# Seven output products in the last block of a hybrid decoder layer too

## The reference

```python
h = rmsnorm(x, norm_g)
proj = h @ w_in                       # 1024 -> q, k, v, gk_lr, gate_g, u, gate_p, q_m, gate_m
o_gla  = rmsnorm(gla_chunked(q, k, v, gk), gla_norm_g) * silu(gate_g)   # 4 heads, 512 channels
o_pool = (pooled @ pool_w) * pool_scale * silu(gate_p)                  # 256 channels
o_mem  = memory_attention(q_m, mem_n, w_mem_kv) * silu(gate_m)          # 256 channels
mixed = concat([o_gla, o_pool, o_mem])                                   # 4096 x 1024
x = x + mixed @ w_out
return rmsnorm(x, final_g)
```

## Time and profile before

| | us |
|---|---|
| median of 3 runs | 1352.45 (1351.65 to 1354.74) |
| the profiled execution | 1352.88 |
| its span, first to last instruction | 1351.1 |
| TensorE busy | 1328.5 |
| VectorE busy | 921.9 |
| ScalarE busy | 817.1 |
| GpSimd busy | 450.7 |
| block 14 starts on TensorE | 1163.36 |
| block 15 (the last) starts | 1242.49 |
| the tail's first matmul | 1324.42 |

### The profile page before, as it was taken

How to read it: one execution, slowest core, us unless ns; L and a number is a source line. 1 busy time by engine, 2 the same in 40 slices (tenths; PEclk the granted TensorE clock), 3 DMA queues, 4 the chain that set the end, 5 groups by cost and what they waited for, 6 DMA issues and landing times.

```text
span 1351.1 us, 35800 instructions
## 1 busy us (share of the span) xinstructions
PE 1328.5 (98%) x14667; PEld 1003.7 (74%) x14667; DVE 921.9 (68%) x1664; ACT 817.1 (60%) x1481; POOL 450.7 (33%) x353
## 2 busy tenths in 40 slices
PE   6999999999999999999999999999999999999998
PEld 5788668577695877859687695968769596886954
DVE  6886667575656757666676857667685766758556
ACT  7886645655647466565655656566574756657353
POOL 2111164136522335243353432335343233534100
PEclk9999999999999999999999999999999999999999
DMA  9575656664673847747595877768596675858631
GB/s 386 190 209 200 243 187 216 209 227 192 216 256 115 330 155 240 260 125 300 186 305 173 280 256 212 263 186 307 183 280 246 211 267 185 311 188 280 251 92 49
DMA packets 155997, 302.92 MB, mean 224 GB/s; under 512 B 76112, under 2 KB 93776, under 8 KB 152656
## 3 DMA queue, kind: packets, MB, share of 16 engines
q1 hardware_dynamic: 155136, 299.75, 65.4%
q10 hardware_dynamic: 720, 1.06, 0.2%
HBM read 249.39 MB, written 34.60 MB: 210 GB/s over the span
## 4 chain that ended last, share of the span: by engine, by line
PE 87%; DVE 5%; ACT 4%; issue 2%; DMA 2%; SPq 0%; ACTq 0%; DVEq 0%
PE bank L863 28%; PE bank L822 21%; PE bank L936 11%; PE bank L842 10%; PE bank L1088 2%; PE bank L1114 2%; PE bank L1108 2%; DVE arena L1955 2%; PE bank L1179 1%; PE bank L1211 1%; ACT arena L1423 1%; PE bank L1099 1%; PE bank L877 1%; PE bank L1131 1%; PE bank L1072 1%
## 5 line engine op out<-in xcount | busy, mean ns | idle before, releaser
L863 PE MATMUL bank<-arena,ring 128*128 128x128 f16 x4032 | 239.0, 219 | 0.5
L863 PE MATMUL bank<-arena,wres 128*128 128x128 f16 x4032 | 237.0, 219 | 0.6 <-DVE arena L1966 0.5
L863 PEld LDWEIGHTS bank<-arena,ring 128*128 128x128 f16 x4032 | 228.9, 98 | 5.5 <-DVE arena L1856 2.4
L863 PEld LDWEIGHTS bank<-arena,wres 128*128 128x128 f16 x4032 | 227.7, 98 | 3.2 <-issue 2.1
L822 PE MATMUL bank<-wv,arena 128*128 128x512 f16 x768 | 168.7, 379 | 0.2 <-DVE wv L1842 0.2
L2457 POOL TENSOR_TENSOR arena<-arena 128x1024 f16<-128x1024 f32 x32 | 70.1, 2212 | 235.8 <-ACT arena L1287 192.7
L822 PE MATMUL bank<-ring,arena 128*128 128x512 f16 x672 | 148.7, 379 | 0.0
L2449 POOL TENSOR_TENSOR arena<-arena 128x1024 f32<-128x1024 f32 (+2 forms) x42 | 64.9, 1545 | 231.9 <-ACT arena L1269 229.7
L822 PEld LDWEIGHTS bank<-wv,arena 128*128 128x128 f16 x768 | 75.0, 98 | 87.6 <-DVE wv L1842 0.4
L936 PE MATMUL bank<-ring,arena 128*128 128x512 f16 x576 | 129.6, 379 | 0.3
L822 PEld LDWEIGHTS bank<-ring,arena 128*128 128x128 f16 x672 | 64.8, 98 | 77.2 <-issue 3.0
(11 more groups left out here) (293 smaller groups left out, 2372.1 us busy)
## 6 DMA issues: line engine op xcount, KB each, us to landing
ring<-out_parts SPq DMA_DIRECT2D x104, 512.0 KB, 4.9
ring<-gate_parts SPq DMA_DIRECT2D x92, 512.0 KB, 7.7
ring<-side_parts SPq DMA_DIRECT2D x92, 512.0 KB, 6.9
ring<-out_sums SPq DMA_DIRECT2D x64, 512.0 KB, 5.0
arena<-in_xt SPq DMA_DIRECT2D x16, 1024.0 KB, 6.1
arena<-in_x SPq DMA_DIRECT2D x32, 512.0 KB, 5.2
out<-arena SPq DMA_DIRECT2D x31, 512.0 KB, 3.0
arena<-in_w_out SPq DMA_DIRECT2D x24, 512.0 KB, 4.7
```

The costliest lines, as they stand in the source:

```text
L863: mm = nc.tensor.matmul(ap, w[:, p, k, j * P:(j + 1) * P], x_part(r, b)[:, k, :], start=fresh and j == 0 and k == 0 and n == 0, stop=k == ...
```

## The change

The last block uses the seven products as well. In the diff: `is_seven` is true for it; SP fills the slots with the plain parts of w_out for the tail, as products end (the branch `if last`), left columns (h = 0) first; TensorE's tail takes in part 0 the left halves of both rows first; VectorE does states 2 and 3 of the last block ahead of p_norm of pairs 2 and 3; its adds 6, 7 and 8 come at the place of `rows(2)`, and add 9 in the tail; the head sums wait for add 5 too; the counts in the waits are carried over. Cut to its core:

```diff
 def loads(kind, i, s):
+    if kind == "last":
+        return loads("out" if s < 2 else "more", i, s) + 1
...
         def is_seven(i, last):
-            return not last and (not isinstance(i, int) or i >= SEVEN)
+            return not isinstance(i, int) or i >= SEVEN
...
                     sums_in(6, T4)
                     sp.wait_ge(pe_out, out_made(i) + 4)
+                    if last:
+                        out_in(((0, 1), (0, 2)))
+                        sp.wait_ge(pe_out, out_made(i) + 5)
+                        out_in(((0, 3), (0, 0)))
+                        store(i - 1, 0)
+                        sp.wait_ge(pe_out, out_made(i) + 6)
+                        out_in(((1, 2), (1, 1)))
+                        sp.wait_ge(pe_out, out_made(i) + 7)
+                        out_in(((1, 3), (1, 0)))
+                        sp.wait_ge(d_store, 16 * (2 * i - 1))
+                        store(i - 1, 1)
+                        return
                     gates_in((0, 1))
...
                     if is_whole(i) or last:
                         pe.wait_ge(o_sq, 2 * i + p + 1)
+                        if last:
+                            pe.wait_ge(y_add, rows_added(i) + 5)
...
-                        for m in ((0, 1), (2, 3), (4, 5), (6,))[n]:
+                        for m in ((0, 1), (2, 3), (4,) if last else (4, 5), (6,))[n]:
                             out_seven(i, m)
...
                     head_ms(0)
                     head_ms(1)
-                    out_proj(i - 1, 3, i, half_sum)
+                    out_seven(i, 5)
+                    half_sum()
+                    out_seven(i, 6)
...
             def tail(n):
-                for part, banks in enumerate(((4, 5, 2, 3), (6, 7, 0, 1))):
-                    for q, b in enumerate(banks):
-                        t, h = q // 2, q % 2
+                for part, places in enumerate((((4, 0, 0), (2, 1, 0), (5, 0, 1), (3, 1, 1)),
+                                               ((6, 0, 0), (7, 0, 1), (0, 1, 0), (1, 1, 1)))):
+                    for q, (b, t, h) in enumerate(places):
...
                             g = k + 4 - 4 * part
+                            if k % 2 == 0:
+                                s = WO_SLOT[h][g // 2]
+                                pe.wait_ge(d_slot[s], 16 * loads("last", n - 1, s))
...
                 state(0)
                 state(1)
+                if last:
+                    state(2)
+                    state(3)
                 p_norm(2)
                 p_norm(3)
...
                     add_seven(i, 4)
                     add_seven(i, 5)
                     pool_gate()
-                    add_seven(i, 6)
-                    add_seven(i, 7)
-                    add_seven(i, 8)
+                    if not last:
+                        add_seven(i, 6)
+                        add_seven(i, 7)
+                        add_seven(i, 8)
                     norm_rows(i - 1, 0, rows_added(i) + 5, y0)
...
                 if last:
                     nc.vector.tensor_reduce(mmax[:, 1:2], mixed[:, 0:4, :], AX.XY, ALU.max,
                                             apply_absolute_value=True).then_inc(mmax_ok, 1)
-                    rows(2)
+                    for m in (6, 7, 8):
+                        add_seven(i, m)
...
             def tail(n):
-                add_rows(n - 2, 3)
+                add_seven(n - 1, 9)
                 mixed_scale(n - 1, sc_last)
```

More of the change, by code:

```diff
@@ L593, in store @@
                 sp.wait_ge(y_ok, j * NT + t + 1)
-                row = y0 if t == 0 and j + 1 >= SEVEN and j + 1 < NB - 1 else yb
+                row = y0 if t == 0 and j + 1 >= SEVEN else yb
                 sp.dma_start(out[bass.ds(j * TB + t * P, P), :], row).then_inc(d_store, 16)
@@ L1201, in tail @@
                         if b < 2:
-                            pe.wait_ge(y_add, rows_added(n - 1) + 3 + b)
+                            pe.wait_ge(y_add, rows_added(n - 1) + (7, 9)[b])
                         if part == 1 and q == 3:
@@ L1206, in tail @@
                             if q == 0 and k % 2 == 0:
-                                pe.wait_ge(m_hi, mixed_split(n - 1) + 2 + 2 * part + k // 2)
-                                pe.wait_ge(m_lo, mixed_split(n - 1) + 2 + 2 * part + k // 2)
+                                pe.wait_ge(m_hi, mixed_split(n) + 1 + 2 * part + k // 2)
+                                pe.wait_ge(m_lo, mixed_split(n) + 1 + 2 * part + k // 2)
                             g = k + 4 - 4 * part
+                            if k % 2 == 0:
+                                s = WO_SLOT[h][g // 2]
+                                pe.wait_ge(d_slot[s], 16 * loads("last", n - 1, s))
                             for j, (p, r) in enumerate(((0, 0), (0, 1), (1, 0))):
@@ L1690, in step @@
                 if is_seven(i, last):
-                    x_plain(i + 1)
+                    if not last:
+                        x_plain(i + 1)
                     norm_y(i - 1, 0, rows_added(i) + 5, y0)
@@ L1743, in tail @@
                                          scale=s_m).then_inc(m_hi, 1)
-                norm_y(n - 2, 1, rows_added(n - 1) + 4)
-                added, norms = rows_added(n - 1) + 4, 6 * (n - 1)
+                norm_y(n - 2, 1, rows_added(n))
+                added, norms = rows_added(n), 6 * (n - 1)
                 act.wait_ge(y_add, added + 2)
@@ L2308, in step @@
                     rows(1)
-                state(2)
-                state(3)
+                if not last:
+                    state(2)
+                    state(3)
                 if is_seven(i, last):
@@ L2360, in step @@
                     for k in (4, 6):
-                        dve.wait_ge(m_hi, mixed_split(i) + k // 2)
+                        dve.wait_ge(m_hi, mixed_split(i + 1) + k // 2 - 1)
                         nc.vector.scalar_tensor_tensor(last_mhl[:, 1, k:k + 2, :], mixed[:, k:k + 2, :], s_half,
@@ L2384, in tail @@
             def tail(n):
-                add_rows(n - 2, 3)
+                add_seven(n - 1, 9)
                 mixed_scale(n - 1, sc_last)
                 for k in (0, 2):
-                    dve.wait_ge(m_hi, mixed_split(n - 1) + 4 + k // 2)
+                    dve.wait_ge(m_hi, mixed_split(n) + 3 + k // 2)
                     nc.vector.scalar_tensor_tensor(last_mhl[:, 1, k:k + 2, :], mixed[:, k:k + 2, :], s_m,
                                                    last_mhl[:, 0, k:k + 2, :], ALU.mult, ALU.subtract).then_inc(m_lo, 1)
-                norm_rows(n - 2, 1, rows_added(n - 1) + 4)
+                norm_rows(n - 2, 1, rows_added(n))
                 dve.wait_ge(half_st, 5)
-                for q, b in enumerate((4, 5, 2, 3)):
-                    t, c = q // 2, slice(512 * (q % 2), 512 * (q % 2) + 512)
-                    if q % 2 == 0:
+                for q, b in enumerate((4, 2, 5, 3)):
+                    t, c = q % 2, slice(512 * (q // 2), 512 * (q // 2) + 512)
+                    if q < 2:
                         dve.wait_ge(d_tail[t], 16)
-                    dve.wait_ge(pe_out, out_made(n - 1) + 5 + q)
+                    dve.wait_ge(pe_out, out_made(n) + 1 + q)
                     nc.vector.scalar_tensor_tensor(yt[t][:, c], bank[b][:, :], sc_half, yt[t][:, c], ALU.mult,
@@ L2412, in tail @@
                                                 ALU.add).then_inc(y_gain, 1)
-                    dve.wait_ge(y_half, min(q, 3) + 1)
-                    dve.wait_ge(pe_out, out_made(n - 1) + 9 + q)
+                    dve.wait_ge(y_half, (1, 3, 3, 4, 4)[q])
+                    dve.wait_ge(pe_out, out_made(n) + 5 + q)
                     nc.vector.scalar_tensor_tensor(yt[t][:, c], bank[b][:, 0:c.stop - c.start], sc_last, yt[t][:, c],
@@ L2581, in step @@
                     mixed_sums(i)
-                    pool.wait_ge(x_sq, i + 2)
-                    fold_rows(3 * (i + 1))
+                    if not last:
+                        pool.wait_ge(x_sq, i + 2)
+                        fold_rows(3 * (i + 1))
                 elif not second and not last:
```

## The result

The changed kernel takes 1358.82 us in the median (1358.01 to 1359.95, 6 runs) against 1352.05 us before (6 runs; one of these took 6119.14 us, a value that no trace explains; without it their median is 1351.65). The ratio is 1.0047, with a 95% interval of 1.0036 to 1.0057: 6.4 us slower, 4.9 to 7.7. The forecast was 1359.5 with a range of 1356.2 to 1361.5, and "slower" had a chance of 0.93.

The account below looks back on a forecast made before the run. TensorE, busy 98% of the span, was taken as the bound. Terms -2.59, +0.75, +6.85 and -0.49 gave +4.52 us; with 2.5 for the clock +7.0, so 1359.5 us, range 1356.2 to 1361.5.

Parts of the forecast that it names:

- The saved product: TensorE, last block: one of eight half-row products removed, 2.59 us saved, first head output at 1309.10 instead of 1311.69.
- The memory product: TensorE, last block: waits 0.75 us for the last transposes, behind the moved states; bounds nothing and 1.1 us.
- The wait of product 6: TensorE ahead of product 6: waits 6.85 us for the block's eighth add, now behind the second maximum on VectorE.
- The clock: TensorE after that wait: 5.0 us of work at half speed, 2.5 us lost; bounds nothing and 4.6 us.
- The tail: Last block's tail products: reordering and the late refill of slots 5 and 6 cost nothing.
- The sum: Whole last block: tail starts 4.52 us later, plus 2.5 us for the clock, +7.0 us.
- the one without the clock's fall: Ahead of product 6: the wait comes but the clock holds, +4.5 us, 1357.0; chance 0.12.
- The one with late slots: In the tail: slots 5 and 6 land late, another 2.1 us, 1361.6; chance 0.06.
- The third rival: Ahead of product 6: no wait, its add count already reached by earlier adds, 1350.6 us; chance 0.04.

Follow-up runs that it names:

- add8_early_recip: add8_early with the reciprocals of memory pairs 2 and 3 ahead of states 2 and 3: 1349.26 us, ratio 0.9981 to the kernel before.
- states_late: The changed kernel with states 2 and 3 back at their old place behind add 3: 1359.07 us, ratio 1.0049 to the kernel before.
- add8_early: The changed kernel with add 8 moved behind add 5 and product 6 waiting for six adds, not eight: 1350.19 us, ratio 0.9986 to the kernel before.
- add8_first_late: The changed kernel with add 8 ahead of adds 6 and 7, behind the second maximum, product 6 waiting for six adds: 1357.92 us, ratio 1.0041.
- longer_wait: The changed kernel with an unread 2.3 us maximum on VectorE ahead of adds 6 to 8: 1360.85 us, ratio 1.0067 to the kernel before.
- warm_filler: The changed kernel with 26 unused matmuls between the half sum and product 6: 1356.65 us, ratio 1.0035 to the kernel before.
- half_first: add8_early_recip with two low halves ahead of head 1 and the tail's first product in bank 2: 1349.21 us, ratio 0.9976 to the kernel before.

## Why the prediction was right, point by point

- The saved product: the first head output was due at 1309.10 and came at 1308.09 + 1.01 = 1309.10. Splits, sums and refills hidden, as costed.
- The memory product: due at 1313.5, came at 1312.42 + 1.01 = 1313.43. The profile names no releaser for this wait; that the moved states cause it is shown by add8_early_recip and states_late.
- The wait of product 6: 6.85 forecast; 7.02 measured as idle time, and 7.17 counted as the forecast does, from the start at which product 6 was due (1318.26 + 0.14). The adds started at 1323.05 + 1.01 = 1324.06 (1324.15 forecast), took 2.25 us instead of 2.06 (2.25 in all four profiles with the order 6, 7, 8 and 2.05 with add 8 first; why is open), and 0.27 us passed to the matmul instead of 0.14. The mechanism is shown by add8_early (gone with the add's place), add8_first_late and longer_wait (shorter and longer with it).
- The clock: the fall came, and it costs, as warm_filler shows. Its size is the term that was off: 2.5 us forecast, from 5.0 us of work at the low level at the start of the kernel; 2.9 us of work and 1.45 us lost in the profiled execution. In other kernels' profiles the low level lasted 4.25, 4.4 and 4.8 us of work (add8_first_late, longer_wait, states_late), and product 6 was 2.1, 2.2 and 2.3 us too long: the 5.0 lies at the upper end, and the profiled execution had a short one. It is also the fastest of its six runs. So part of the closeness of 1359.5 to the median rests on a length that varies, which the forecast took from one place.
- The tail: refill and order at nothing, as costed. 18.26 us against 18.27, and the two last loads took 4.2 us in the changed kernel, where 4.7 were taken and 6.6 were free. What follows the first tail matmul is 26.91 us instead of 26.68; the last VectorE instruction of the chain starts 22.85 us behind it in both, so these 0.2 us lie behind that, in the end of the final norm and the last store.
- The sum: tail 6.18 us later than before, counted from the block's start (7.0 forecast). By terms that is -2.59 for the product, +0.66 for the memory product, +7.17 for the wait, -0.49 as forecast, +1.43 for the clock. Of the difference of 0.84, 1.07 is the clock and 0.09 the memory product, less 0.32 for the longer adds and handover. The medians differ by 6.8 us, the ratio gives 6.4.

Of the rivals, the one without the clock's fall (+4.5) lies just below the interval of 4.9 to 7.7 us, and the windows rule it out. The one with late slots did not happen in this kernel. The forecast's reason against it, an empty queue, held because of the wait: the queue was busy until about 1325, the DMA share is 0.00 from 1327 on, and these two loads were issued at 1329.78. Without the wait the same two loads took 7.1 us (add8_early), 6.8 (add8_early_recip) and 7.2 (half_first), and in half_first one is waited for. The row of the changed kernel, to set beside that of half_first:

```profile
ring<-out_parts SPq DMA_DIRECT2D x2, 512.0 KB, 4.2
```

The third rival, no wait at all, was priced at 1350.6 us. Its condition did not hold, but add8_early, which makes it hold, took 1350.19.

## What to carry to other kernels

When an operation moves back in one engine's list, look up every wait that counts it, not only its own inputs: here an add that frees a bank went behind the critical chain with two others that had reason to be there (they read product 5, which now comes late), and a saving of 2.6 us became a loss of 6.4. A wait of several microseconds on TensorE is to be costed with the slower matmuls behind it: here 1.4 to 2.3 us on top of waits of 5.5 to 9.2 us. And a transfer that is hidden in a kernel with a wait is to be costed again for the kernel without it.

## What the hardware showed that I had not expected

The same wait does not always cost the same through the clock. The granted clock fell 2.2 us after the last matmul at the end of the kernel before, 3.1 us after it in the changed kernel and 5.0 in states_late, though the last two have the same wait of 7.02 us. In all, the low level lasted 6.8 us in the changed kernel, in add8_first_late and in states_late, and 10.2 us in longer_wait. In the three with 6.8 us, how much of it falls on work depends on how long before the resume it begins: 3.9 us before in the changed kernel leaves 2.9 us of slow work, 2.6 us before in add8_first_late 4.25, and 2.1 us before in states_late 4.8. That makes product 6 longer by 1.43 us in the first and by 2.34 in the last (4.93 instead of 2.59), and it is why the wait shortened by 1.5 us brought only 0.9 in the profile. What sets the start and the 10.2 us is open. The windows of states_late show the late fall (first row, a mean of both levels: the fall is at about 1325.2), nearly the whole of product 6 at the low level, and the return at about 1332.1 (last row):

```profile
1325.00:1326.00 1.00, 0.00 (x0) 0.62 0.35 139
...
1331.00:1332.00 1.00, 1.00 (x4) 0.50 0.00 0
...
1332.00:1332.50 0.50, 0.50 (x4) 0.93 0.00 0
```

The last two transposes of the last block took 3.2 us to land in add8_early_recip and 4.1 in half_first, with the same program up to there. The memory product came 0.46 us later for it, counted from the block's start (70.74 against 70.28), 0.39 of it idle.
